# The norms of the delta rule's q and k computed in the stream of the convolutions, and a shorter beginning of a head's preparation

## The reference, cut to what matters

```
qkv = silu(causal_dwconv(concat(dn_q, dn_k, dn_v), dn_conv_w))      # 24 tiles of 128 channels x 512 tokens
q_a, k_a = l2_norm(q), l2_norm(k)      # x * rsqrt(sum(x*x over the 128 columns of a head) + 1e-6)
qc = q_a * 128 ** -0.5
gc = cumsum(g in chunks of 64);  decay = exp(gc_i - gc_j) for i >= j
a_mat = strictly lower part of (k_beta k^T) * decay
[u, w] = solve(I + a_mat, [v_beta, k_beta * exp(gc)])
intra = lower part of (qc k^T) * decay;  q_e = qc * exp(gc)
then a recurrence over the 8 chunks, with q_e, intra, u, w and the decayed k
```

## Time and profile before

| what | before |
|---|---|
| median of 3 runs | 2564.14 us |
| the profiled execution, its own time | 2568.02 us |
| its span | 2566.2 us |
| PE / DVE / ACT / POOL busy | 92 / 42 / 36 / 27 % |
| mean granted TensorE clock | 0.954 of full speed |
| longest part of the chain that ended last | PE 74 % |

### The profile page before, as it was taken

The page is one execution under the profiler, slowest core; times in us unless marked ns, Lnnn a source line. Parts: engine busy times, 40 slices in busy tenths (PEclk is TensorE's granted clock), DMA queues, the critical chain, the costliest instruction groups (busy, mean ns, idle before and its releaser), DMA issues.

```text
span 2566.2 us, 27004 instructions
## 1 busy us (share of the span) xinstructions
PE 2361.6 (92%) x10928; PEld 1894.9 (74%) x10928; DVE 1085.4 (42%) x1580; ACT 924.4 (36%) x1350; POOL 701.7 (27%) x416
## 2 busy tenths in 40 slices
PE   8798989999798899899999888999999999999996
PEld 4577877985566677688888676787777777888875
DVE  2576655454433332433321499513444243322333
ACT  2544423223432432533322332334552433322334
POOL 1141144002011125322223232321232353432332
PEclk9898989999899899899999898999999999999998
DMA  8222223121122124333333422232211322333341
GB/s 261 74 66 70 70 58 99 50 82 33 37 62 68 43 82 119 103 102 95 95 96 96 123 82 66 82 92 82 82 58 58 114 83 82 107 91 99 99 123 50
DMA packets 347983, 220.66 MB, mean 86 GB/s; under 512 B 18393, under 2 KB 327244, under 8 KB 347860
## 3 DMA queue, kind: packets, MB, share of 16 engines
q1 hardware_dynamic: 338462, 202.31, 27.3%
q10 hardware_dynamic: 9398, 16.62, 1.9%
HBM read 210.49 MB, written 8.41 MB: 85 GB/s over the span
## 4 chain that ended last, share of the span: by engine, by line
PE 74%; DVE 11%; ACT 8%; POOL 2%; issue 2%; DMA 2%; ACTq 0%; SPq 0%; DVEq 0%; POOLq 0%
PE ps L342 73%; DVE arena L368 4%; ACT arena L357 3%; DVE arena L360 2%; ACT scr L357 1%; DVE scr L368 1%; PE ps L345 1%; ACT whi L357 1%; POOL arena L360 1%; DMA wraw<-in_w_in_dram 1%; POOL wlo L360 1%; ACT L353 1%; DVE scr L360 1%; DVE wlo L360 1%; DVE arena L365 1%
## 5 line engine op out<-in xcount | busy, mean ns | idle before, releaser
L360 POOL TENSOR_TENSOR wlo<-wraw,whi 128x1024 fp32r<-128x1024 f32 (+1 forms) x163 | 390.8, 2398 | 1229.4 <-ACT whi L357 1229.4
L342 PE MATMUL ps<-hhi,whi 128*128 128x512 f32 x1664 | 678.3, 408 | 50.6 <-POOL wlo L360 31.2
L342 PE MATMUL ps<-hlo,whi 128*128 128x512 f32 x1664 | 661.9, 398 | 0.0
L342 PE MATMUL ps<-hhi,wlo 128*128 128x512 f32 x1664 | 661.2, 397 | 0.0
L357 ACT ACTIVATE whi<-wraw 128x1024 fp32r<-128x1024 f32 (+1 forms) x328 | 340.7, 1040 | 347.8 <-PE ps L342 294.7
L342 PEld LDWEIGHTS ps<-hhi,whi 128*128 128x128 f32 x1664 | 322.1, 194 | 131.6 <-issue 44.5
L342 PE MATMUL ps<-arena 128*128 128x128 f32 (+4 forms) x2304 | 337.1, 302 | 40.0 <-ACT arena L357 17.5
L342 PEld LDWEIGHTS ps<-hlo,whi 128*128 128x128 f32 x1664 | 322.0, 194 | 68.5 <-issue 3.7
L342 PEld LDWEIGHTS ps<-hhi,wlo 128*128 128x128 f32 x1664 | 320.8, 193 | 70.0
L360 DVE TENSOR_TENSOR wlo<-wraw,whi 128x1024 fp32r<-128x1024 f32 (+2 forms) x165 | 213.3, 1292 | 372.6 <-ACT whi L357 372.4
L342 PEld LDWEIGHTS ps<-arena 128*128 128x128 f32 x2304 | 291.4, 198 | 70.0 <-ACT arena L357 22.0
(11 more groups left out here) (190 smaller groups left out, 2729.1 us busy)
## 6 DMA issues: line engine op xcount, KB each, us to landing
wraw<-in_w_in_dram SPq DMA_DIRECT2D x99, 512.0 KB, 3.9
wraw<-in_w_ff_dram SPq DMA_DIRECT2D x64, 512.0 KB, 4.0
wraw<-in_ffn_w_up_dram SPq DMA_DIRECT2D x44, 512.0 KB, 3.8
wraw<-in_w_ada_dram SPq DMA_DIRECT2D x32, 512.0 KB, 3.9
wraw<-in_w_gate_dram SPq DMA_DIRECT2D x32, 512.0 KB, 3.9
arena<-in_w_ada_dram SPq DMA_DIRECT2D x8, 1024.0 KB, 11.5
wraw<-in_ffn_w_down_dram SPq DMA_DIRECT2D x16, 512.0 KB, 4.1
wraw<-in_w_branch_dram SPq DMA_DIRECT2D x16, 512.0 KB, 3.5
```

The source lines that it names most:

```text
L342: return pe.e.matmul(o, l, r, start=start, stop=stop)
L360: return q.e.tensor_tensor(o, a, b, op)
```

## The change

The norms leave `prep`. When the silu of q or k of a head is issued, ACT also squares it (`norm_square`), into buffers of its own (`NSQ`). Before each third linear (place n of `CONV` with n % 3 == 1) the sums, the logarithms and the exps of the head before follow (`norm_sum`, `norm_root`), and before the next linear the scaling on DVE (`norm_scale`); a pair may begin when its second head is scaled. `small_proj` does this for head 7. In `prep` the steps before the levels are arranged anew: g and kk in step 0; qk and b on PE, and kk, am, b0, xt0, at on DVE, in step 2; kt and x, and kd and kb, in step 4; the levels from step 6. ACT's eg and dm and DVE's d are in step 0. A pair has 18 steps and an empty one, and the weave gives 76 side steps to 24 main steps.

```diff
+        def NSQ(x, h):
+            return A[:, 24 + h, :] if x == "q" else A[:, 32 + h // 2, :]
             def flush(self):
                 for c in self.due:
                     self.dn_silu(c)
-                    self.have.add(c)
+                    if c < 16:
+                        self.norm_square("qk"[c // 8], c % 8)
                 self.due.clear()
...
+            def norm_step(self, n):
+                if n % 3 == 1 and n > 1:
+                    for x in "qk":
+                        self.norm_sum(x, n // 3 - 1)
+                    for x in "qk":
+                        self.norm_root(x, n // 3 - 1)
+                if n % 3 == 2 and n > 2:
+                    for x in "qk":
+                        self.norm_scale(x, n // 3 - 1)
+                    self.have.add(("normal", n // 3 - 1))
...
-            weave(chain(first, paced(f.small_proj(), more)), f.prep_pairs(), 30, 100)
+            weave(chain(first, paced(f.small_proj(), more)), f.prep_pairs(), 24, 76)
...
+            def norm_sum(self, x, h):                                   # Tensor
+                bk = PA.take("dn", h, x)
+                pe.wait_ge(*PA.free("dn", h, x))
+                pe.wait_ge(*at("dp_act", "sq", x, h))
+                mm(bk[:, :], ones, NSQ(x, h), True, True).then_inc(*inc("dp_mm", "sq", x, h))
+                PA.put(("dn", h, x), "dp_act", "ln", x, h)
...
+            def norm_root(self, x, h):                                  # Scalar
+                o = NSQ(x, h)
+                ac.wait_ge(*at("dp_mm", "sq", x, h))
+                act(o, PA.of("dn", h, x)[:, :], ACT.Ln, bias=kcol(K_EPS)).then_inc(*inc("dp_act", "ln", x, h))
+                ac.wait_ge(*at("dp_act", "ln", x, h))
+                act(o, o, ACT.Exp, scale=-0.5, bias=kcol(K_QB) if x == "q" else 0.0).then_inc(*inc("dp_act", "ri", x, h))
...
+            def norm_scale(self, x, h):                                 # Vector
+                v = A[:, h if x == "q" else 8 + h, :]
+                ve.wait_ge(*at("dp_act", "ri", x, h))
+                tt(ve, v, v, NSQ(x, h), ALU.mult).then_inc(*inc("dp_ve", x, h))
...
-                while 16 + h not in self.have:                          # prep, all four engines
+                while ("normal", h | 1) not in self.have:
                     yield
```

More of the change, by code:

```diff
@@ L706, in qkv @@
             def qkv(self, more):
-                for h, b, c in CONV:
+                for n, (h, b, c) in enumerate(CONV):
                     if c not in (0, 8):
+                        self.norm_step(n)
                         yield from self.linear(f"dn{c}", self.ev_dn(c))
@@ L731, in small_proj @@
                 for j in range(4):
+                    if j < 3:
+                        self.norm_step(24 + j)
                     yield from self.linear(f"qr{j}", self.ev_qr(j))
@@ L804, in build @@
             norm2 = norm3 = spill2 = conv_start = att_start = att_zero = gla_start = xr_load = mg_split = nothing
-            ff2_start = norm5 = last_turns = ab = dn_conv = dn_taps = dn_silu = ada_add = ada_end = nothing
+            ff2_start = norm5 = last_turns = ab = dn_conv = dn_taps = dn_silu = norm_square = norm_sum = norm_root = norm_scale = ada_add = ada_end = nothing
             ev_ck = ev_qn = ev_z = ev_gd = ev_gm = ev_ya = ev_yb = ev_wo = ev_ple = ev_fa = ev_fv = ev_fd = nothing
@@ L1115, in prep @@
                 blk = [slice(b * P, (b + 1) * P) for b in range(4)]
-                while 16 + h not in self.have:
+                while ("normal", h | 1) not in self.have:
                     yield
[L1118 to L1126, removed]
                 bk = PA.take("dn", h, "g")
@@ L1140, in prep @@
                 PA.put(("dn", h, "kk"), "dp_ve", "kk", h)
+                yield
+                yield
                 bk = PA.take("dn", h, "qk")
@@ L1683, in token_cols, with norm_square @@
                 act(TD, bk[:, 64:96], ACT.Exp).then_inc(*inc("ab_act", "td"))
+            def norm_square(self, x, h):
+                if x == "k" and h % 2:
+                    ac.wait_ge(*at("dp_ve", "k", h - 1))
+                ac.wait_ge(*at("qkv", h if x == "q" else 8 + h))
+                act(NSQ(x, h), A[:, h if x == "q" else 8 + h, :], ACT.Square).then_inc(*inc("dp_act", "sq", x, h))
+            def norm_root(self, x, h):
[4 more added lines that the diff above has]
+                act(o, o, ACT.Exp, scale=-0.5, bias=kcol(K_QB) if x == "q" else 0.0).then_inc(*inc("dp_act", "ri", x, h))
             def prep(self, h, w):
@@ L3009, in prep @@
                 cp(po, EGL[:, h, :], EG[:, 63:512:64]).then_inc(*inc("dp_po", "egl", h))
+                po.wait_ge(*at("dp_ve", "at", h))
+                tt(po, AT_[h], AT_[h], spread(CST[:, C_AM:C_AM + 64], 1, 4), ALU.mult).then_inc(*inc("dp_po", "am", h))
+                yield
                 yield
```

47 lines of the change are left out of this document (11 added, 36 removed).

## The result

The changed kernel takes 2568.97 us, the median of 10 runs (2566.07 to 2573.31); the kernel before took 2564.2 us beside it (10 runs, 2562.6 to 2566.08). The ratio is 1.0018, 95% interval [1.0009, 1.0026]. So it is 4.8 us slower, where the forecast was 2 us faster. The profiled execution took 2573.31 us, its span 2571.4 us, at a mean granted clock of 0.954 as before. The clock is no accident of that execution: it is 0.954 to 0.958 in the ten runs of the changed kernel and 0.953 to 0.958 in 19 runs of the kernel before, the middle one 0.956 in both.

The account below looks back on a forecast made before the run. TensorE was taken to bound the kernel, busy 92%; the preparation lost idle time and slow clock. Waits grow 7.8 us, the clock returns 9.5: about -2 us, so 2562 against 2564.1; range 2551 to 2572.

Parts of the forecast that it names:

- The removed waits: TensorE's idle time in the 352.0 us preparation before the change, all counted as removed: 30.7 us.
- Waits of steps 0 to 2: At each pair's start TensorE waits 1.25 and 2.6 us for banks: 3.9 in pairs 0 to 2, 1.5 in pair 3.
- The sum behind kt's bank: Second sum waits until VectorE's kb frees kt's bank: 4.1 us in pair 0, 3.8 in pair 1, 0.9 in pair 2.
- Rival 2: The second sum's 4 us wait drops the clock again in pairs 0 and 1: 2572 us, chance 0.23.
- The smaller waits: Step 7 1.9 us, u 1.6, 0.25 in each of pairs 0 to 2, and 4.5 in front.
- Step 7: TensorE waits for ScalarE's copies behind the silu's table load: 1.9 us in pairs 0 to 2, ends 1.5 and 2.5.
- the front: Before pair 0, linears 7 and 8 wait 1.0 and 3.5 us for late weights: 4.5 us.
- Pair 3: Waits of the last pair's steps 0 to 2, whose linear is one of small_proj: 1.5 us.
- The clock: Slow-clock time in the preparation falls from 15 us to 5 to 6, a gain of 9.5; bounds 3 and 15.
- u's wait: At step 17 u waits for VectorE's vb behind the taps: 1.6 us in pairs 0 and 1, lower end nothing.
- the three signs: Wrong if the sums by ones don't wait, the stretch's clock share stays 0.94, or TensorE's waits sum below 32 us.
- The tables' rule: Each table switch costs 2.7 us, 1.4 more at six places: 8 us, time 2570, chance no more than 0.05.

Follow-up runs that it names:

- waits filled: Changed kernel with TensorE repeating the first product of q and k once and b six times in heads 0, 2 and 4: 2569.39 us, ratio 1.0016.
- vb earlier: Changed kernel with v transposed and vb computed on VectorE one step earlier: 2565.24 us, ratio 1.0003.
- steps spread only: Changed kernel with side steps dealt to linears by a written list, kk's tile a step earlier and at first in its step on VectorE: 2543.46 us, ratio 0.9908.
- the order alone: Kernel before with the new order of a pair's steps, norms staying in the preparation: 2572.68 us, ratio 1.0034.
- the move alone: Kernel before with norms moved into the stream of the convolutions, the rest of a pair in its old order: 2562.64 us, ratio 0.9995.
- mask later: Changed kernel with GpSimd's mask of at moved behind its last step of the levels: 2562.77 us, ratio 0.9991.
- four waits mended: Changed kernel with dm later, vb earlier, the mask later, and kt behind the levels' first product with kd and kb two steps later: 2550.87 us, ratio 0.9950.
- The fastest version: Changed kernel with dm, vb, mask and kt edits, plus side steps by written list and VectorE's kk and at moves: 2535.92 us, ratio 0.9881.

## Why the prediction was wrong, by its own steps

**The removed waits: right.** Idle time before is 30.7 us. The slow clock before was put at 15 us; busy time less 304 us gives 17.3.

**Waits of steps 0 to 2: right.** Said 1.25 and 2.6 us, measured 1.11 and 2.42, in all three pairs; pair 3 said 1.5, measured 0.90.

**The sum behind kt's bank: the bound right by luck, the wait not.** It was to be free at T+22.1 in pair 0, T the end of the linear: 139.5 + 22.1 = 161.6, and the row has 161.65. In pair 1 T+21.8 was said (the terms named there add up to 21.3 with `ada_add` at 1.40), and the row, 253.24, is T+22.8. TensorE came at T+20.4 and not at T+18.0 in pair 0, since the products and the linear before it ran slower and waited 0.3 less: 1.72 and 1.80 us of wait, where 4.1 and 3.8 were said. But in pair 0 the bound itself is two errors that cancel. VectorE in order of time:
```profile
154.54 1.90 DVE L368 SCALAR_TENSOR_TENSOR scr<-wraw,mod,scr 128x512 f32<-128x512 f32 x2
158.09 2.32 DVE L368 SCALAR_TENSOR_TENSOR scr<-ps,colv,scr 128x511 f32<-128x511 f32 x3 [1.65 <-ACT scr L357]
160.32 2.48 DVE L360 TENSOR_TENSOR arena<-ps,small 128x512 f32<-128x512 f32 x4
```
`ada_add` took 1.90 us and not 3.51, and then VectorE waited 1.65 us for ScalarE's copy of the linear that ran slow and ended at 157.32. In "waits filled", where this linear runs at full clock, VectorE has no such wait and the sum starts at T+20.5 (160.23, T 139.69).

Rival 2 took this wait, at over 3 us, for what would bring the clock down a second time. The wait stayed below that, and the linear behind it (162.22 to 168.26) ran at full clock, so the rival's mechanism didn't occur here, although its 2572 us is near the result. In other kernels it did: behind waits of 2.36 (vb earlier), 2.74 (waits filled), 2.82 and 2.92 us (steps spread only) at this sum, the linear took 7.07 to 7.64 us.

**The smaller waits: right in sum, two of them off.** Step 7 waits 2.08 us three times (said 1.9, ends 1.5 and 2.5), u 2.05 twice (said 1.6), 0.25 three times, `ada_end` 0.93 (said 2.3), the sum behind it 1.72 (said 0.9), the front 0.79 + 2.48 = 3.3 (said 4.5). There are 21 table loads, as said. In sum idle is 36.0, said 38.5.

**Pair 3: a wait missed.** 1.5 us were said; measured are 0.90 + 2.34 + 0.33 + 1.05 = 4.6 (the last two were 0.34 and 0.45 before). I followed VectorE, ScalarE and the banks, but not GpSimd's queue, where the mask that waits for the last `at` stands ahead of the low weights. Moving the mask removed the wait.

**The clock: the step that failed.** "I charge 0.5 each there, 2 in pair 2, 2.5 in front: 5 to 6, against 15." By pair, predicted against measured, idle and slow clock together (measured from the rows at low clock less the same at full clock):

| | predicted | measured |
|---|---|---|
| front | 4.5 + 2.5 = 7.0 | 3.3 + 1.6 = 4.9 |
| pair 0 | 11.75 + 0.5 = 12.3 | 9.6 + 4.3 = 13.9 |
| pair 1 | 11.45 + 0.5 = 12.0 | 9.7 + 4.8 = 14.5 |
| pair 2 | 9.25 + 2 = 11.3 | 8.5 + 5.5 = 14.0 |
| pair 3 | 1.5 | 4.6 |
| all | 44.0 | 51.9 |

(36.0 + 16.4 = 52.4 by the busy time of the whole stretch; the rows leave out 0.5.)

Three things are in it. First, the slow time was to be taken out of the sum's wait in pairs 0 and 1, because VectorE bounds that stretch. In pair 1 it was: VectorE starts the taps (249.67) without a wait. In pair 0 it was not, for the most part: of 2.6 us of slow time before the sum, 1.0 came out of its wait and 1.6 moved it back (T+22.1 against T+20.5 in "waits filled"), since VectorE's taps wait for the slow linear itself. Second, behind u's wait the clock falls once more, and 24 products take 4.5 us instead of 2.8, in pairs 0 and 1, with nothing behind them to absorb it; I had priced u's wait by its idle time alone. These 3.3 us are the part that another execution may not show (7 of 12 places in the profiles). Third, in pair 2 no wait of VectorE's absorbs the slow time, and it covers the second qk (0.9), b (0.3), `ada_end` (1.7) and the linear (2.6): 5.5, not 2. I had taken one linear at 2.3 as the price of one fall of the clock and left out the small products that run slow with it. So the slow clock is 16.4 us as against 17.3, and the 9.5 us that should have paid for the 7.8 of added waits were 0.9. The sum is 5.3 - 0.9 = +4.4 us. None of the three signs that I had named as proof of being wrong came true to the letter: the stretch's granted clock is 0.95, between the 0.94 of before and the 0.97 that was said, the sums do wait, and idle time is over 32 us. The sign to name was TensorE's busy time in the stretch, which tells what the clock gives back and stayed at 320.

The waits' causes are shown by runs of one edit each for the second qk, the sum, u and the low weights; the one at step 7 was changed only together with others. That the new order costs is shown by the order alone (+7.6 us against the kernel before beside it). That a linear between steps 0 and 2 is worth 25.5 us is shown by the spread list; as this is five times what the change lost, and the pairs' starts waited longer before the change, it shows what can be won there and not where the 4.8 us came from. By the rows they came from the new waits at the sums, step 7, u and the low weights, which outweigh what the starts lost; the waits at u (2.06 and 2.05 us) and most of those at step 7 (1.55 three times) stand in the move alone too, those at the sums and for pair 3's low weights do not. The move of the norms itself costs nothing that can be measured, and it gains nothing by itself either.

The tables' rule of the Trainium skill, which I weighed at 2570 us, comes out near the measured time by accident. In pair 0 of the changed kernel, ScalarE in order of time:
```profile
168.30 0.69 ACT L357 ACTIVATE scr<-ps,colv 128x512 f32<-128x512 f32 x1 [2.39 <-PE ps L342]
169.00 1.28 ACT L357 ACT_TABLE_LOAD   x1
170.30 0.63 ACT L357 ACTIVATE arena<-scr 128x512 f32<-128x512 f32 x1
170.96 0.63 ACT L357 ACTIVATE arena<-arena 128x512 f32<-128x512 f32 x1
171.50 1.06 ACT L357 ACTIVATE arena<-ps 128x512 f32<-128x512 f32 x2
```
The load begins 0.01 us behind the copy and the silu 0.02 us behind the load. By the Trainium skill ("ScalarE: Activation LUTs", "What ACT_TABLE_LOAD costs") about 1.38 us of drain would stand there too. With it the wait at step 7 would be about 3.5 us (an estimate, 2.08 + 1.38); the trace has 2.08, so no drain shows here.

**What stays open.** What brings the clock down isn't settled. Idle time of 1.1 and 2.4 us in short order at a pair's start was followed by it every time. Behind a single wait of about 2 us it went either way: slow in 7 of 12 places behind the 2.05 us at u, in 1 of 15 behind the 2.08 us at step 7 (five profiles; the one is in "mask later", 7.25 us for 48 products), and behind the 2.3 us for the low weights in pair 3 slow in "vb earlier" and "waits filled" (7.32 and 7.31) and not in the changed kernel. Filling two waits in part with small matmuls did not prevent it in two pairs of three, and one linear was slow without any wait before it (below). So the length of the wait alone doesn't tell it.

## What to carry to other kernels

When steps are made fewer, look at which of them now follow each other without covering work, and deal them out so that one unit of the large matmuls stands between each handing over and its use; that was worth more here (25.5 us) than four waits mended (18). Price a wait of TensorE with what runs slow behind it, small products included, and only then take off what another engine's bound absorbs; first look whether that engine itself waits for the unit that runs slow. Follow every queue that feeds the next large unit through the new order, also the one of the engine that is busy for a quarter of the time.

## What the runs showed of the hardware

The clock fell once behind small matmuls with no idle time at all. The fastest version, pair 2, TensorE in order of time:
```profile
304.78 0.50 PE L342 MATMUL ps<-gb,sel 40*128 40x512 f32 x1
305.21 1.16 PE L342 MATMUL ps<-arena 128*128 128x128 f32 x8
306.29 0.49 PE L342 MATMUL ps<-gb,sel 40*128 40x512 f32 x1
306.71 1.16 PE L342 MATMUL ps<-arena 128*128 128x128 f32 x8
307.71 1.84 PE L342 MATMUL ps<-cst,scr 128*128 128x1 f32 x16
309.42 0.53 PE L342 MATMUL ps<-hhi,whi 128*128 128x512 f32 x1
309.74 0.63 PE L342 MATMUL ps<-hlo,whi 128*128 128x512 f32 x1
```
Eight matmuls of this linear take 0.58 to 0.63 us, and it lasts 7.33 us. Ahead of it stood 4.6 us of gates, products of 128 columns and `ada_end`'s single columns, each row joined to the next. It is no rule: the same rows in pair 2 of "steps spread only" (312.78 to 317.42) were followed by a linear at full clock (5.71 us), and so were 10 us of such products in the kernel before (197.32 to 207.30, the linear 5.73).

A wait that is taken away can be worth more than its length: 3.9 us less waiting at the second qk brought 7.2 us in the changed kernel, and in the kernel before the same edit brought 6.9 us with the idle time unchanged. The same wait can also cost more or less from one execution to the next, by whether the clock falls behind it: 24 products behind 2.05 us took 4.5 or 2.92 us.
